# The inter-chunk product of a Mamba-2 scan: one fp32 product becomes three fp32r products of operands split by ScalarE and VectorE

## The chip, the cores and the metric

One NeuronCore of a Trainium2 chip runs the whole program in one launch. The metric is the device time of that launch in microseconds; each kernel is timed several times and the median is taken. Engines are called by the profile's names: PE (TensorE, matrix products), ACT (ScalarE), DVE (VectorE), POOL (GpSimd) and SP (SyncE, which issues the loads of the weights).

## What is computed

A decoder of two layers over 256 tokens of width 2048, all in fp32. The first layer is a Mamba-2 mixer, the second a sliding-window attention; each is followed by a squared-ReLU MLP. The change lies in the state-space scan of the mixer, which the reference does in two chunks of 128 tokens:

```python
def step(state, inp):
    xdt_c, dA_c, b_c, c_c = inp
    cs = jnp.cumsum(dA_c, axis=1)
    seg = cs[:, :, None] - cs[:, None, :]
    decay = jnp.exp(jnp.where(causal[None, :, :, None, None], seg, -jnp.inf))
    cb = jnp.einsum('bign,bjgn->bgij', c_c, b_c)
    y_intra = jnp.einsum('bgij,bijgh,bjghp->bighp', cb, decay, xdt_c)
    y_inter = jnp.einsum('bign,bghpn->bighp', c_c, state) * jnp.exp(cs)[..., None]
    to_end = jnp.exp(cs[:, -1:] - cs)
    new_state = (state * jnp.exp(cs[:, -1])[..., None, None]
                 + jnp.einsum('bjgn,bjgh,bjghp->bghpn', b_c, to_end, xdt_c))
    return new_state, y_intra + y_inter
```

With two chunks and a zero state at the start only `y_inter` of the second chunk is not zero. It is what the first token half carries into the second. There are eight groups of eight heads (64 columns each).

## The kernel before

Weights stream from HBM in chunks of 128x1024 numbers. Every fp32 product of weights is done as three fp32r products (high by high, low by high, high by low). So ACT rounds each chunk into `whi` (`split_weights`, L838) and DVE writes the rest into `wlo` (L1270); a ring of eight such slots (`RING`) runs up to six chunks ahead of PE (`LEAD`), and the raw chunks have four buffers (`RAW`). On ACT and DVE one call of `step()` splits one chunk, and the order of all other work between the steps is written out by hand in `group` of each engine. The semaphores `w_split` (chunk ready) and `w_used` (chunk used) tie the streams to PE.

The mixer goes group by group. On PE, `group(par, prev)` makes six row tiles of the current group (`row_tile(i % 2, actA)`, lines L453 and L459, into PSUM banks 0 and 1 by turns) and then a block of z columns (`column_block`, L478 to L480). Between them stands the scan of the previous group:

- behind row tile 0, `s1`: transposes of x, and C times B of the tokens (`cb`) into bank 6 (L593, L594)
- behind row tile 3, `s4_both`: the inter-chunk product `s4` (L610, 128x128 by 128x512 in fp32), then the intra-chunk products `intra(0, 5)` and `intra(1, 7)` (L602), which wait on `m_ready`
- inside the column block, the transposes of the normed result (`s67`)

Row tile 4 goes into bank 0 again, so `fill(0)` waits until DVE has taken row tile 2 out of it, in `conv_sum` of `conv(2)` (L1393).

On ACT, `cross` (L913) takes half a row tile out, `tanh` (L923) serves the silu, and `decay(c)` makes the decay matrix `em` of a token half: eight ReLUs (L940) and an exp (L944). On DVE, `d1(c)` scales x by dt (L1428, L1430) and `d1(1)` also makes `xde` (L1434), the moving operand of `s4`; `bc_out` takes `cb` out of bank 6, two masked tiles (L1440) and a copy (L1441) which is the weight of `s4`; `d23(c)` multiplies `em` by the masked `cb` (L1446) and signals `m_ready`.

The last (eighth) group's scan runs in the first block of the out projection, `slab(actA, ..., after={3: [s4], 5: [lambda: intra(1, 7)], 7: [s67]})`, beside `split_y` of DVE and ACT.

Of the kernel before, what the change touches and what calls it, by code (L numbers as in the profile page):

```python
# [23 lines left out]
F32 = mybir.dt.float32  # L24
F32R = mybir.dt.float32r
ACT = mybir.ActivationFunctionType
ALU = mybir.AluOpType
AX = mybir.AxisListType

P = 128  # L30
T = 256
NH = T // P
# [4 lines left out]
GH = 8  # L37
HD = 64
GW = GH * HD
# [90 lines left out]
def build(nc, t, out):  # L130
# [24 lines left out]
    z_tanh_done = nc.alloc_semaphore("z_tanh_done")  # L155
    xdt_ready = nc.alloc_semaphore("xdt_ready")
    m_ready = nc.alloc_semaphore("m_ready")
    y_ready = nc.alloc_semaphore("y_ready")
    y_squared = nc.alloc_semaphore("y_squared")
    rstd_ready = nc.alloc_semaphore("rstd_ready")  # L160
# [17 lines left out]
    full = [nc.alloc_semaphore(f"full{b}") for b in range(8)]  # L178
# [60 lines left out]
    def region(start, limit):  # L239
        pos = [start]  # L240

        def put(name, shape, dtype=F32):
            x = place(name, shape, dtype, pos[0])
            pos[0] += (int(np.prod(shape[1:])) * 4 + 31) // 32 * 32
            assert pos[0] <= limit, (name, pos[0] - limit)
            return x
        return put
# [6 lines left out]
    xD = put("xD", [P, NH, GW])  # L254
    xin = place("xin", [P, NH, D], F32, res_at)
    put = region(scr, end)
    xT = put("xT", [P, 2, 6, T])
    xpad = put("xpad", [P, 2, 3 + T + 1])
    xh = put("xh", [P, 2, T])
    thb = put("thb", [P, 2, T])  # L260
    yb = put("yb", [P, NH, GW])
    zs = put("zs", [P, NH, GW])
    xde = put("xde", [P, GW])
    bcb = put("bcb", [P, 3, P])
    st = put("st", [P, GW])

    put = region(y_at, y_at + KT * 2 * T * 4)
    kst = put("kst", [P, K_END])
# [71 lines left out]
    with block:  # L340
# [76 lines left out]
        def _(e):  # L417
# [187 lines left out]
                last.then_inc(full[b], C.up(full[b]))  # L605

            def s4():
                e.wait_ge(xdt_ready, C.next(xdt_ready))
                fill(4)
                e.matmul(ps[:, 4, :], bcb[:, 1, :], xde[:, :], start=True, stop=True).then_inc(full[4], C.up(full[4]))  # L610
                intra(0, 5)

            def s4_both():
# [214 lines left out]
        def _(e):  # L828
# [11 lines left out]
            def step():  # L840


                C.n[w_used] += 1
                if C.n[w_hi_done] < TOTAL and C.any(w_used, back=RING - 1 - LEAD):
                    e.wait_ge(w_used, C.now(w_used, back=RING - 1 - LEAD))
                split_weights()
# [74 lines left out]
            def tanh(i):  # L921
                e.wait_ge(conv_done, C.next(conv_done))
                e.activation(thb[:, i % 2, :], xh[:, i % 2, :], ACT.Tanh).then_inc(tanh_done, C.up(tanh_done))  # L923
# [4 lines left out]
                    e.activation(yb[:, c, :], ps[:, 2 + c, :], ACT.Tanh, scale=0.5).then_inc(  # L928
                        z_tanh_done, C.up(z_tanh_done))

            def a1():
                C.n[full[6]] += 1
                C.n[free[6]] += 1

            def decay(c, par):
                if c == 0:
                    e.wait_ge(rows_in, C.next(rows_in))
                    e.wait_ge(group_sums, C.next(group_sums))
                for h in range(GH):
                    last = e.activation(em[:, c, h * P:(h + 1) * P], csb[:, h, c * P:(c + 1) * P], ACT.Relu,  # L940
                                        bias=csg[:, par, c, h:h + 1], scale=-1.0)
                last.then_inc(clamped, C.up(clamped))
                e.wait_ge(clamped, C.now(clamped))
                e.activation(em[:, c, :], em[:, c, :], ACT.Exp, scale=-1.0).then_inc(decayed, C.up(decayed))  # L944
# [60 lines left out]
            def group(par):  # L1005
                step()
                z_tanh()
                step()
                step()
                cross(0)  # L1010
                step()
                tanh(0)
                a1()
                step()
                cross(1)
                decay(0, par)
                step()
                tanh(1)
                step()
                cross(2)  # L1020
                decay(1, par)
                step()
                tanh(2)
                step()
                cross(3)
                step()
                tanh(3)
                step()
                cross(4)
                step()  # L1030
                tanh(4)
                square(0)
                step()
                cross(5)
                step()
                tanh(5)
                square(1)
                step()
                scale_y()
                for _ in range(5):  # L1040
                    step()
# [15 lines left out]
            split_y(0, range(2))  # L1057
            z_tanh()
            split_y(0, range(2, 4))
            a1()  # L1060
            step()
            decay(0, 1)
            step()
            decay(1, 1)
            step()
# [194 lines left out]
        def _(e):  # L1260
# [12 lines left out]
            def step():  # L1273
                C.n[w_used] += 1
                split_weights()
# [160 lines left out]

            def bc_out():
                e.wait_ge(full[6], C.next(full[6]))
                for c in range(NH):
                    e.tensor_tensor(bcb[:, 2 * c, :], ps[:, 6, 2 * c * P:(2 * c + 1) * P], tri[:, :], ALU.mult)  # L1440
                e.tensor_copy(bcb[:, 1, :], ps[:, 6, P:2 * P]).then_inc(free[6], C.up(free[6]))  # L1441

            def d23(c):
                e.wait_ge(decayed, C.next(decayed))
                x = em[:, c, :].rearrange("p (h n) -> p h n", h=GH)
                e.tensor_tensor(x, x, bcb[:, 2 * c, :].unsqueeze(1).broadcast_to([P, GH, P]), ALU.mult).then_inc(  # L1446
                    m_ready, C.up(m_ready))

            def gate(c):
# [74 lines left out]
            def group(g, par):  # L1524

                step()
                e.tensor_copy(cwg[:, par, :], cw[:, bass.ds(g * 30, 30)]).then_inc(dve_step, C.up(dve_step))
                e.wait_ge(dve_step, C.now(dve_step))
                step()
                z_out()  # L1530
                step()
                conv(0, par)
                bc_out()
                step()
                d1(0, g - 1)
                step()
                conv(1, par)
                silu(0, par)
                d1(1, g - 1)
                step()  # L1540
                d23(0)
                d23(1)
                step()
                conv(2, par)
                silu(1, par)
                step()
                step()
                conv(3, par)
                silu(2, par)
                step()  # L1550
                d4()
                step()
                conv(4, par)
                silu(3, par)
                step()
                d5(g - 1)
                step()
                conv(5, par)
                silu(4, par)
                step()  # L1560
                silu(5, par)
                for _ in range(5):
                    step()
                d8(0, g - 1)
                step()
                d8(1, g - 1)
# [46 lines left out]

            g7 = NG - 1
            step()
            split_y(0, {1: bc_out})
            z_out()
            d1(0, g7)
            d1(1, g7)
            step()  # L1620
            d23(0)
            step()
            d23(1)
            step()
# [480 lines left out]
```

## Time and profile before

| what | value |
|---|---|
| time, median of 3 runs | 2387.52 us (2387.07 to 2387.99) |
| span of the profiled execution | 2386.3 us |
| PE busy | 2368.3 us (99%) |
| DVE busy | 1588.6 us (67%) |
| ACT busy | 1140.5 us (48%) |
| rate of the DMA, mean | 191 GB/s |

The span runs from the first to the last instruction of the profiled execution; the three timed runs lie 0.8 to 1.7 us above it, which is what lies around the span. A busy share says nothing of who waits for whom: for that there are the views of waits, of the chain of work, and the timelines of a stretch. In a timeline each row has the start in us from the span's start, the duration in us, engine, line, operation, output and inputs, shapes and how many instructions were merged.

### The profile page before, as it was taken

Reading aid. Unit: us, or ns where it says so; the run is one execution under the profiler, and the core shown is the slowest. Engines: PE = TensorE matmul, PEld = TensorE weight load, DVE = VectorE, ACT = ScalarE, POOL = GpSimd, SP = SyncE. Lnnn points to the kernel's source line nnn. Section 1 sums busy time; section 2 is a strip of 40 time slices with the busy share of each in tenths; the row PEclk is TensorE's granted clock in tenths of the full one; section 3 lists DMA queues with packets and bytes.
Section 4 is the critical chain, followed back from the end, with each engine's and each line's share of the span. In section 5 each row is a group of like instructions: output and inputs, shape, how many; then the busy total and the mean of one; then the engine's idle time right before and its main releaser. Section 6 shows DMA issues by size and latency. Waiting matters only on the chain.

```text
span 2386.3 us, 32914 instructions
## 1 busy us (share of the span) xinstructions
PE 2368.3 (99%) x12818; PEld 2005.7 (84%) x12818; DVE 1588.6 (67%) x2171; ACT 1140.5 (48%) x1670; POOL 40.1 (2%) x85
## 2 busy tenths in 40 slices
PE   9999999999999999999999999999999999999998
PEld 8888888888888888888888888778888888888886
DVE  7888888885568556556556577876864654655655
ACT  5555555564355344445344354554543443443441
POOL 0000000000000000000000000000000000000000
PEclk9999999999999999999999999999999999999999
DMA  8766666656567666666666646336776666666663
GB/s 233 230 195 194 188 191 190 189 169 239 193 186 235 210 187 190 198 186 187 200 186 190 199 150 209 120 122 198 201 234 189 188 198 182 194 197 189 190 196 108
DMA packets 487828, 455.11 MB, mean 191 GB/s; under 512 B 13792, under 2 KB 360080, under 8 KB 485392
## 3 DMA queue, kind: packets, MB, share of 16 engines
q1 hardware_dynamic: 484608, 433.51, 60.3%
q0 software_dynamic: 3088, 19.79, 2.3%
q8 instruction: 90, 1.47, 0.3%
q14 instruction: 42, 0.34, 0.0%
HBM read 450.55 MB, written 2.16 MB: 190 GB/s over the span
## 4 chain that ended last, share of the span: by engine, by line
PE 93%; DVE 3%; DMA 2%; ACT 1%; issue 1%; SPq 0%; POOL 0%; DVEq 0%; ACTq 0%
PE ps L453 24%; PE ps L478 16%; PE ps L480 15%; PE ps L479 15%; PE ps L459 12%; PE ps L511 2%; PE ps L509 2%; PE ps L510 2%; PE ps L530 1%; DVE wlo L1270 1%; DMA raw<-in_a_w_in 1%; ACT whi L838 1%; PE ps L746 1%; PE ps L602 1%; PE ps L716 0%
## 5 line engine op out<-in xcount | busy, mean ns | idle before, releaser
L1270 DVE TENSOR_TENSOR wlo<-raw,whi 128x1024 fp32r<-128x1024 f32 x817 | 994.3, 1222 | 656.6 <-ACT whi L838 656.1
L838 ACT ACTIVATE whi<-raw 128x1024 fp32r<-128x1024 f32 x817 | 859.4, 1056 | 853.9 <-PE ps L480 461.2
L453 PE MATMUL ps<-actA,whi 128*128 128x512 f32 x2704 | 648.2, 392 | 0.8 <-DVE wlo L1270 0.5
L453 PEld LDWEIGHTS ps<-actA,whi 128*128 128x128 f32 x2704 | 497.2, 188 | 98.4 <-issue 0.7
L478 PE MATMUL ps<-whi,actB 128*128 128x512 f32 x1056 | 412.8, 391 | 0.1
L479 PE MATMUL ps<-wlo,actB 128*128 128x512 f32 x1056 | 411.1, 389 | 0.0
L480 PE MATMUL ps<-whi,actB 128*128 128x512 f32 x1056 | 411.1, 389 | 0.0
L459 PEld LDWEIGHTS ps<-actA,wlo 128*128 128x128 f32 x2704 | 347.2, 191 | 13.4
L459 PE MATMUL ps<-actA,wlo 128*128 128x256 f32 x2704 | 351.4, 283 | 0.0
L478 PEld LDWEIGHTS ps<-whi,actB 128*128 128x128 f32 x1056 | 198.3, 188 | 43.0 <-issue 1.3
L480 PEld LDWEIGHTS ps<-whi,actB 128*128 128x128 f32 x1056 | 198.3, 188 | 41.3
L479 PEld LDWEIGHTS ps<-wlo,actB 128*128 128x128 f32 x1056 | 198.3, 188 | 40.3
L478 PE MATMUL ps<-whi,actA 128*128 128x512 f32 x544 | 216.0, 397 | 1.7 <-DVE actA L1282 1.7
L480 PE MATMUL ps<-whi,actA 128*128 128x512 f32 x544 | 212.1, 390 | 0.0
L479 PE MATMUL ps<-wlo,actA 128*128 128x512 f32 x544 | 212.1, 390 | 0.0
L478 PEld LDWEIGHTS ps<-whi,actA 128*128 128x128 f32 x544 | 102.2, 188 | 24.3 <-issue 3.2
L480 PEld LDWEIGHTS ps<-whi,actA 128*128 128x128 f32 x544 | 102.1, 188 | 21.7
L479 PEld LDWEIGHTS ps<-wlo,actA 128*128 128x128 f32 x544 | 102.3, 188 | 19.8
L852 ACT ACTIVATE actB<-fsq 128x256 fp32r<-128x256 f32 x120 | 50.2, 418 | 111.7 <-DVE fsq L1748 111.7
L1599 DVE TENSOR_TENSOR res<-ps,res 128x512 f32<-128x512 f32 x80 | 51.9, 686 | 63.0 <-PE ps L511 32.6
L923 ACT ACTIVATE thb<-xh 128x256 f32<-128x256 f32 x48 | 19.9, 415 | 125.9 <-DVE xh L1410 125.9
L1748 DVE SCALAR_TENSOR_TENSOR fsq<-fb 128x256 f32<-128x256 f32 x120 | 51.0, 425 | 4.1
(215 smaller groups left out, 1674.3 us busy)
## 6 DMA issues: line engine op xcount, KB each, us to landing
raw<-in_mlp_w SPq DMA_DIRECT2D x512, 512.0 KB, 4.2
raw<-in_a_w_in SPq DMA_DIRECT2D x162, 512.0 KB, 4.4
raw<-in_a_w_out SPq DMA_DIRECT2D x64, 512.0 KB, 4.8
raw<-in_b_w_q SPq DMA_DIRECT2D x32, 512.0 KB, 5.2
raw<-in_b_w_o SPq DMA_DIRECT2D x32, 512.0 KB, 3.9
csb<-cs_rows POOLq DMA_DIRECT2D x8, 1024.0 KB, 6.7
raw<-in_kv_w SPq DMA_DIRECT2D x16, 512.0 KB, 3.8
gb<-in_ln_g POOLq DMA_DIRECT2D x4, 1024.0 KB, 7.3
```

The lines of the kernel that those rows point to most:

```text
L453: e.matmul(ps[:, b, :], whi[:, s, k * P:(k + 1) * P], act[:, kt, :, :].rearrange("p a n -> p (a n)"), start=(kt == 0), stop=False)
L459: last = e.matmul(ps[:, b, T:2 * T], wlo[:, slots[half], k * P:(k + 1) * P], act[:, kt, 0, :], start=False, stop=(kt == KT - 1))
L478: e.matmul(ps[:, b0 + h, :], act[:, kt, 0, tk], whi[:, s, w], start=(kt == 0), stop=False)
L479: e.matmul(ps[:, b0 + h, :], act[:, kt, 0, tk], wlo[:, s, w], start=False, stop=False)
L480: last = e.matmul(ps[:, b0 + h, :], act[:, kt, 1, tk], whi[:, s, w], start=False, stop=(kt == KT - 1))
L509: e.matmul(ps[:, b0 + h, :], act[:, kt, 0, tk], hi_w, start=(kt == 0), stop=False)
L510: e.matmul(ps[:, b0 + h, :], act[:, kt, 0, tk], lo_w, start=False, stop=False)
L838: e.activation(whi[:, s, :], raw[:, r, :], ACT.Copy).then_inc(w_hi_done, C.up(w_hi_done))
L852: e.activation(dst, src, ACT.Copy).then_inc(act_hi_done, C.up(act_hi_done))
L1270: e.tensor_tensor(wlo[:, s, :], raw[:, r, :], whi[:, s, :].bitcast(F32), ALU.subtract).then_inc(w_split, C.up(w_split))
L1599: ins = e.tensor_tensor(r, ps[:, b, :], r, ALU.add)
L1748: e.scalar_tensor_tensor(fsq[:, i % 2, :], fb[:, i % 2, :], 0.0, fb[:, i % 2, :], ALU.max, ALU.mult).then_inc(f_squared, C.up(f_squared))
```

## The change

- `s4` on PE becomes three fp32r products into bank 4: `cbh` by `xeh`, `cbh` by `xel`, `cbl` by `xeh`. It waits on `xe_split` instead of `xdt_ready`.
- ACT gets `cb_hi` (high part of the 128x128 `cb`, out of PSUM bank 6) and `xe_hi` (high part of the 128x512 `xde`). In a group `cb_hi` stands ahead of `tanh(0)` and `xe_hi` behind `tanh(1)`; in the last group `xe_hi` stands behind `decay(0, 1)`.
- DVE gets `xe_lo` (the rest of `xde`, 128x512) between `d23(0)` and `d23(1)`. In `bc_out` the copy of `cb` becomes a subtraction, and it waits on `cb_hi_done`.
- In the last group `bc_out` moves from behind piece 1 of `split_y` to behind piece 3.
- Some tiles move in SBUF; `xel` lies over `xde`.

```diff
             def s4():
-                e.wait_ge(xdt_ready, C.next(xdt_ready))
+                e.wait_ge(xe_split, C.next(xe_split))
                 fill(4)
-                e.matmul(ps[:, 4, :], bcb[:, 1, :], xde[:, :], start=True, stop=True).then_inc(full[4], C.up(full[4]))
+                e.matmul(ps[:, 4, :], cbh[:, :], xeh[:, :], start=True, stop=False)
+                e.matmul(ps[:, 4, :], cbh[:, :], xel[:, :], start=False, stop=False)
+                e.matmul(ps[:, 4, :], cbl[:, :], xeh[:, :], start=False, stop=True).then_inc(full[4], C.up(full[4]))
                 intra(0, 5)
...
-            def a1():
-                C.n[full[6]] += 1
+            def cb_hi():
+                e.wait_ge(full[6], C.next(full[6]))
+                e.activation(cbh[:, :], ps[:, 6, P:2 * P], ACT.Copy).then_inc(cb_hi_done, C.up(cb_hi_done))
                 C.n[free[6]] += 1
+
+            def xe_hi():
+                e.wait_ge(xdt_ready, C.next(xdt_ready))
+                e.activation(xeh[:, :], xde[:, :], ACT.Copy).then_inc(xe_hi_done, C.up(xe_hi_done))
...
                 step()
+                cb_hi()
                 tanh(0)
-                a1()
                 step()
                 cross(1)
                 decay(0, par)
                 step()
                 tanh(1)
+                xe_hi()
                 step()
                 cross(2)
                 decay(1, par)
...
-            a1()
+            cb_hi()
             step()
             decay(0, 1)
+            xe_hi()
             step()
             decay(1, 1)
...
             def bc_out():
                 e.wait_ge(full[6], C.next(full[6]))
+                e.wait_ge(cb_hi_done, C.next(cb_hi_done))
                 for c in range(NH):
-                    e.tensor_tensor(bcb[:, 2 * c, :], ps[:, 6, 2 * c * P:(2 * c + 1) * P], tri[:, :], ALU.mult)
-                e.tensor_copy(bcb[:, 1, :], ps[:, 6, P:2 * P]).then_inc(free[6], C.up(free[6]))
+                    e.tensor_tensor(bcb[:, c, :], ps[:, 6, 2 * c * P:(2 * c + 1) * P], tri[:, :], ALU.mult)
+                e.tensor_tensor(cbl[:, :], ps[:, 6, P:2 * P], cbh[:, :].bitcast(F32), ALU.subtract).then_inc(
+                    free[6], C.up(free[6]))
+
+            def xe_lo():
+                e.wait_ge(xe_hi_done, C.next(xe_hi_done))
+                e.tensor_tensor(xel[:, :], xde[:, :], xeh[:, :].bitcast(F32), ALU.subtract).then_inc(
+                    xe_split, C.up(xe_split))
...
                 d23(0)
+                xe_lo()
                 d23(1)
...
-            split_y(0, {1: bc_out})
+            split_y(0, {3: bc_out})
             z_out()
             d1(0, g7)
             d1(1, g7)
             step()
             d23(0)
+            xe_lo()
             step()
             d23(1)
```

ACT in the first full group, from the splitting of a chunk behind `decay(0)` on, as the program issues it before (L838 is the rounding of a weight chunk, L923 `tanh`, L913 `cross`, L940 and L944 `decay(1)`; the semaphores waited for stand in brackets):

```order
L838 ACTIVATE whi<-raw 128x1024 [waits loaded1,w_used]
L923 ACTIVATE thb<-xh 128x256 [waits conv_done]
L838 ACTIVATE whi<-raw 128x1024 [waits loaded2,w_used]
L913 ACTIVATE xpad<-ps 128x256 [waits w_used]
L940 ACTIVATE em<-csb,csg 128x128 x8
L944 ACTIVATE em<-em 128x1024 [waits clamped]
L838 ACTIVATE whi<-raw 128x1024 [waits loaded3,w_used]
```

The same place now (line numbers of the changed kernel; L847 rounds a chunk, L932 is `tanh`, L947 `xe_hi`, L922 `cross`, L954 and L958 `decay(1)`):

```order
L847 ACTIVATE whi<-raw 128x1024 [waits loaded1,w_used]
L932 ACTIVATE thb<-xh 128x256 [waits conv_done]
L947 ACTIVATE xeh<-xde 128x512 [waits xdt_ready]
L847 ACTIVATE whi<-raw 128x1024 [waits loaded2,w_used]
L922 ACTIVATE xpad<-ps 128x256 [waits w_used]
L954 ACTIVATE em<-csb,csg 128x128 x8
L958 ACTIVATE em<-em 128x1024 [waits clamped]
```

One instruction has come in, and it waits for a product of DVE (`xdt_ready`); a chunk, `cross` and the whole of `decay(1)` are queued behind it.

PE in the same group before, at `s4_both` (L459 ends row tile 3, L610 is `s4`, L602 the intra-chunk products of the two token halves):

```order
L459 MATMUL ps<-actA,wlo 128x256 x16
L610 MATMUL ps<-xde,bcb 128x512 [waits free4,xdt_ready]
L602 MATMUL ps<-xdt,em 64x64 [waits free5,m_ready]
L602 MATMUL ps<-xdt,em 64x64 x15
L602 MATMUL ps<-xdt,em 64x64 [waits free7,m_ready]
```

And now:

```order
L466 MATMUL ps<-actA,wlo 128x256 x16
L617 MATMUL ps<-xeh,cbh 128x512 [waits free4,xe_split]
L618 MATMUL ps<-xel,cbh 128x512
L619 MATMUL ps<-xeh,cbl 128x512
L609 MATMUL ps<-xdt,em 64x64 [waits free5,m_ready]
L609 MATMUL ps<-xdt,em 64x64 x15
```

One product in the program's order has become three, and the first of them waits for a semaphore that DVE raises later than the old one.

## Rows read from the trace of the kernel before

**Rows 1.** The page: span, granted clock by slice, shares of the last-ending chain

```profile
span 2386.3 us, 32914 instructions
...
PEclk9999999999999999999999999999999999999999
...
PE 93%; DVE 3%; DMA 2%; ACT 1%; issue 1%; SPq 0%; POOL 0%; DVEq 0%; ACTq 0%
```

**Rows 2.** Waits of PE: who for whom, us in total, times, longest

```profile
PE ps L478 <- DVE actA L1282: 1.7, 1, 1.7
...
PE ps L453 <- DVE wlo L1270: 0.5, 1, 0.5
PE ps L453 <- DVE xpad L1393: 0.3, 1, 0.3
```

**Rows 3.** Chain of work, last group's s4: start, us, what

```profile
516.79 0.23 PE ps L480
517.03 0.86 PE ps L610 x2
```

**Rows 4.** Timeline of PE in a middle group

```profile
205.88 0.38 PE L594 MATMUL ps<-xT 128*128 128x128 f32 x2
...
222.83 1.02 PE L610 MATMUL ps<-xde,bcb 128*128 128x512 f32 x2
...
225.79 0.50 PE L453 MATMUL ps<-actA,whi 128*128 128x512 f32 x1
```

**Rows 5.** Timeline of ACT in the same group

```profile
216.63 0.40 ACT L923 ACTIVATE thb<-xh 128x256 f32<-128x256 f32 x1
216.94 1.04 ACT L838 ACTIVATE whi<-raw 128x1024 fp32r<-128x1024 f32 x1
...
220.62 1.06 ACT L944 ACTIVATE em<-em 128x1024 f32<-128x1024 f32 x1
```

**Rows 6.** Timeline of DVE in the same group

```profile
208.40 0.48 DVE L1440 TENSOR_TENSOR bcb<-ps,tri 128x128 f32<-128x128 f32 x2
...
217.13 0.68 DVE L1434 TENSOR_TENSOR xde<-xdt,te 128x512 f32<-128x512 f32 x1
...
221.71 1.23 DVE L1446 TENSOR_TENSOR em<-em,bcb 128x1024 f32<-128x1024 f32 x1 [1.62 <-ACT em L944]
222.85 1.22 DVE L1270 TENSOR_TENSOR wlo<-raw,whi 128x1024 fp32r<-128x1024 f32 x1
223.99 0.42 DVE L1393 TENSOR_TENSOR xpad<-ps,xpad 128x256 f32<-128x256 f32 x1
...
229.00 0.42 DVE L1393 TENSOR_TENSOR xpad<-ps,xpad 128x256 f32<-128x256 f32 x1
```

**Rows 7.** Chain of work, the first group that holds a scan

```profile
102.91 1.13 DVE wlo L1270
104.04 0.34 DVE xpad L1393
...
104.43 1.66 PE ps L453 x6
```

**Rows 8.** Timelines of ACT and DVE, the same group

```profile
96.91 1.04 ACT L838 ACTIVATE whi<-raw 128x1024 fp32r<-128x1024 f32 x1
...
97.19 0.68 DVE L1434 TENSOR_TENSOR xde<-xdt,te 128x512 f32<-128x512 f32 x1
```

**Rows 9.** Groups by line and form: busy us, mean ns, idle before

```profile
L852 ACT ACTIVATE actA<-hf 128x512 fp32r<-128x512 f32 x16 | 10.1, 632 | 11.0 <-DVE hf L1661 10.6
L957 ACT ACTIVATE xdt<-yb,small 128x512 f32<-128x512 f32 x16 | 10.7, 716 | 6.2 <-POOL small L1996 6.2
```

**Rows 10.** Timelines of ACT and DVE in the last group

```profile
512.27 1.04 ACT L838 ACTIVATE whi<-raw 128x1024 fp32r<-128x1024 f32 x1
...
513.13 0.68 DVE L1434 TENSOR_TENSOR xde<-xdt,te 128x512 f32<-128x512 f32 x1
...
514.86 1.22 DVE L1446 TENSOR_TENSOR em<-em,bcb 128x1024 f32<-128x1024 f32 x1
```

More of the change, by code:

```diff
@@ L157, in build @@
     m_ready = nc.alloc_semaphore("m_ready")
+    cb_hi_done = nc.alloc_semaphore("cb_hi_done")
+    xe_hi_done = nc.alloc_semaphore("xe_hi_done")
+    xe_split = nc.alloc_semaphore("xe_split")
     y_ready = nc.alloc_semaphore("y_ready")
@@ L256, in build @@
     put = region(scr, end)
+    st = put("st", [P, GW])
+    xeh = place("xeh", [P, GW], F32R, scr)
+    xde = put("xde", [P, GW])
+    xel = place("xel", [P, GW], F32R, scr + GW * 4)
     xT = put("xT", [P, 2, 6, T])
@@ L262, in build @@
     zs = put("zs", [P, NH, GW])
-    xde = put("xde", [P, GW])
-    bcb = put("bcb", [P, 3, P])
-    st = put("st", [P, GW])
+    bcb = put("bcb", [P, NH, P])
+    cbh = put("cbh", [P, P], F32R)
+    cbl = put("cbl", [P, P], F32R)
     put = region(y_at, y_at + KT * 2 * T * 4)
@@ L1445, in d23 @@
                 x = em[:, c, :].rearrange("p (h n) -> p h n", h=GH)
-                e.tensor_tensor(x, x, bcb[:, 2 * c, :].unsqueeze(1).broadcast_to([P, GH, P]), ALU.mult).then_inc(
+                e.tensor_tensor(x, x, bcb[:, c, :].unsqueeze(1).broadcast_to([P, GH, P]), ALU.mult).then_inc(
                     m_ready, C.up(m_ready))
```

## Prediction

> **What bounds the kernel now.** I read the page first. Of the chain that ended last 93% is PE, and PE is granted its full clock in every slice [rows 1]. So the kernel costs what PE issues, plus the few places where PE waits. The view of PE's waits shows how few there are [rows 2]: once 1.7 us for DVE's `split_y` at the start of the last group's scan, once 0.5 us for a weight chunk, once 0.3 us for DVE's `conv_sum` (L1393). An edit that shortens PE's own work is therefore worth its full size, and an edit on ACT or DVE costs nothing until it makes one of their results later than PE asks for it. The question is how much room each result has, so I read the timelines of a middle group, of the first group with a scan, and of the last.
>
> **What is removed on PE.** The fp32 product is recorded as two matmuls and takes 0.86 us of the chain, while an fp32r product of 512 columns takes 0.23 [rows 3]. Three of these are 0.69, so each `s4` is 0.17 us shorter, and the eight of them 1.4 us. I take the rows' price for the three, since they have the shape of L480; a price that is certain from below is none (0 us saved) and from above 0.23 each, as if one of them vanished into the change of weights.
>
> **What is added on ACT.** `cb_hi` reads `cb` out of PSUM. In the middle group PE has it ready at 206.26 (205.88 + 0.38) [rows 4] and DVE asks for it only at 208.40, in `bc_out` [rows 6]. A copy of 128x128 is smaller than the 0.40 us of `tanh` over 128x256 [rows 5], so 1.7 us of room is left, and it costs nothing. The subtraction that takes the place of the copy in `bc_out` has the shape of the two L1440 beside it, 0.48 us for two; I cost the exchange at nothing, at most 0.1 us.
>
> `xe_hi` is another matter. It waits for `xde` (L1434), and ACT's queue is in order: a weight chunk, `cross(2)` and the whole of `decay(1)` stand behind it. Before, ACT began that chunk (L838) at 216.94, while `xde` is ready only at 217.81 (217.13 + 0.68) [rows 5, 6]. A hand-over between ACT and DVE takes 0.03 us (the exp ends at 221.68, L1446 starts at 221.71 [rows 5, 6]). The copy itself is like L852 from SBUF to fp32r, 128x512, 0.63 us [rows 9], of which 0.09 overlaps the next instruction (`tanh` begins at 216.63, takes 0.40, and the next begins at 216.94). So the chunk begins at 217.81 + 0.03 + 0.54 = 218.38, 1.44 us later. The copy with a scale of the same shape, L957, is 0.72 [rows 9]; the cost could be that, or as little as 0.45 if the overlap were twice as large, and the delay 1.35 to 1.53.
>
> **Who waits for that.** Everything behind it moves by 1.44: the exp of `decay(1)` from 221.68 to 223.12, DVE's L1446, then the weight split L1270, then `conv_sum(2)` (L1393), which ended at 224.41 (223.99 + 0.42) and now ends at 225.85. On DVE these follow one another with no room [rows 6]. PE asks for bank 0, which `conv_sum(2)` empties, at row tile 4, at 225.79 [rows 4]. With 0.05 us from DVE to PE (L1393 ends at 104.38, PE starts at 104.43 [rows 7]) the room was 225.79 - 224.41 - 0.05 = 1.33 us. So PE starts row tile 4 at 225.90, 0.11 us later than before, and the 0.17 won at `s4` just before is lost inside this wait. The bounds of the copy make it 0.02 to 0.20. `xe_lo` on DVE is hidden: it fits into the idle 1.62 us before L1446 [rows 6], and PE needs `xel` only at 222.83 [rows 4]. Between the first scan and the last, the eighth, lie six such groups of the same pattern: 6 x 0.11 = 0.7 us.
>
> **The first group with a scan** has no room: there the chain of work itself runs over `decay(1)`, L1446, L1270 and L1393 into row tile 4 [rows 7]. The same sum gives 97.19 + 0.68 + 0.03 + 0.54 = 98.44 against 96.91 before [rows 8], 1.53 us later, and all of it falls on PE. Its `s4` saving is lost too, since PE then waits longer at the same place.
>
> **The last group.** `xde` is ready at 513.81, and ACT's chunk, which began at 512.27 [rows 10], falls 2.1 us back, plus what `bc_out` behind piece 3 puts in front of `z_out` and `d1` on DVE (three instructions, 0 to 0.6 us). Behind it is `decay(1)`, whose product `intra(1, 7)` stands two chunks, 24 products of 0.23 or 5.4 us, behind `s4`, so this is hidden. What is not hidden is `xe_lo`: it follows L1446, which ends at 516.08 [rows 10], so it ends at 516.7 to 517.3, where PE takes up `s4` at 517.03 [rows 3]. A wait of 0 to 0.4 us against a saving of 0.17: I take +0.1.
>
> **The sum.** 1.53 + 0.66 + 0.1 = +2.3 us on a span of 2386.3 [rows 1]. The timed runs lie 1.2 us above that span in the median, so 2387.5 + 2.3 = 2389.8 us. That is 0.1% and less than the 0.2% (4.8 us) from which a measurement of this kernel tells a difference.
>
> **Rivals.**
>
> (a) *The stall never reaches PE, and the saving stays.* If ACT's queue has more room than I count, for instance because `xe_hi` starts nearer to the end of `tanh(1)`, PE wins 0.17 at each of eight `s4`: 2387.5 - 1.4 = 2386.1. For it speaks that in the middle groups only 0.11 us decides; against it that the first group is on the chain. A mix (middle groups win, first loses) gives 2388. Together 0.22.
>
> (b) *Slower than can be overlooked: DVE's `bc_out` waits for ACT's `cb_hi`.* If ACT comes to `cb_hi` late, `d1` and `xde` come later by as much, and with them `xe_hi`, `decay(1)`, `conv_sum(2)` and row tile 4, in all seven groups. With the forecast at +2.3, a further delay of (4.8 - 2.3) / 7 = 0.36 us in each group decides it. Half a microsecond would give 2389.8 + 3.5 = 2393.3. Against it stand the 1.7 us of room [rows 4, 6]. The same price holds for anything else that adds to the chain, up to the next asker: row tile 5 comes 5.5 us after row tile 4 (16 x 0.23 and 16 of half the width), at about 231.3, and `conv_sum(3)` ends at 229.42 [rows 6], or 230.9 with the delay, so 0.4 us are left there. Chance 0.09.
>
> (c) *The change does not do what it says: a pass costs what half the fp32 product does.* Then three passes take 3 x 0.43 = 1.29 us, 0.43 more than before. In the middle groups PE comes to row tile 4 at 226.22, past the 225.90 of DVE, so the loss is 0.43 there, 1.53 in the first, 0.43 and some wait in the last: 2.6 + 1.5 + 0.6 = 4.7, 2392.2. Against it, every L480 of the same shape is 0.23 [rows 3]. Chance 0.03.
>
> (d) *The clock.* A mechanism of this kernel would be that after the new wait of 1.5 us in the first group the granted clock falls to 1.2 GHz for one row tile; its 5.5 us would take twice that: 2389.8 + 5.5 = 2395.3. Against it: before, PE waited 1.7 us at one place [rows 2] and the granted clock shows 9 in all forty slices [rows 1]. Chance 0.02. The Trainium skill (Perfetto Trace Analysis, Matmul Optimizations) says that TensorE scales its power with its use, so that matmuls have to be issued back to back; by that rule a kernel that trades PE work for PE waits stands to lose. The trace does not bear it out at waits of this length.
>
> **How the numbers follow.** The forecast has 0.64. It lies within 0.2%, as does (a) and most of (c); (b) and (d) are slower, and a little of the forecast's own tail is (0.01). For faster by over 0.2% I find no mechanism, since all that PE can win is 1.4 us; 0.02 is for what I overlooked. So faster 0.02, same 0.86, slower 0.12. The range reaches from (a), 2386.0, to the border of (b), 2393.0.
>
> **What would show it.** In the trace of the changed kernel: three matmuls of 0.23 us spacing at `s4`; ACT's copy `xeh<-xde` beginning 0.03 us after `xde` ends, with ACT idle 0.8 us before it; in the middle groups PE idle some 0.3 us before row tile 4, released by `xpad` of DVE, which PE's waits did not show there before; in the first group about 1.8 us of it. If these waits are absent, (a) holds. If DVE idles before `bcb`, released by ACT's `cbh`, it is (b). The prediction is wrong if PE shows waits for `xe_split` in middle groups, or a weight chunk that comes late because its split stood behind the stalled chunk.

## The result, and the profile after

The changed kernel takes 2393.49 us in the median (2391.09 to 2395.36, 12 runs) against 2387.98 (2387.07 to 2389.46, 12 runs) of the kernel before: a ratio of 1.0021, with a 95% interval of 1.0014 to 1.0028. It is 5.5 us slower, a little over the 4.8 us that the prediction named as 0.2%; the prediction had 2.3 us. The median lies half a microsecond above the predicted range, but the kernel before also measures 0.46 us more here, in 12 runs, than the 2387.52 of three runs that the range was built on: as a difference, 5.5 us is just the distance from 2387.52 to the range's upper end. Two things stand out beside the median. The profiled execution, with a span of 2390.7 us, is 4.4 longer than that of before, so a typical run has about 1 us more than the trace explains. (A timed run lies 1.8 us above its own span, 2392.51 against 2390.7 here; the 0.8 to 1.7 us named before the prediction set timed runs against the span of another execution.) And the runs scatter more: 4.3 us from lowest to highest, against 2.4. That is a weak sign, since longer series of the kernel before (26 to 33 runs, below) span 3.7 to 4.3.

The waits of PE in the changed kernel (L460 is a row tile's product, L609 an intra-chunk product, L485 the column block, L537 the transposes; us in total, times, longest):

```profile
PE ps L460 <- DVE xpad L1409: 2.0, 7, 0.3
PE ps L609 <- DVE em L1469: 1.7, 1, 1.7
PE ps L485 <- DVE actA L1298: 1.4, 1, 1.4
PE ps L537 <- DMA xin<-in_x: 1.2, 2, 1.0
PE ps L537 <- DVE yT L1496: 1.2, 1, 1.2
```

The first row is the forecast one: row tile 4 now waits for `conv_sum(2)` seven times instead of once [rows 2]. The second is the first group with a scan. The last, for `yT`, was not forecast. The same middle group as in [rows 4 to 6], PE first, after the change:

```profile
225.00 0.40 PE L617 MATMUL ps<-xeh,cbh 128*128 128x512 f32 x1
225.24 0.40 PE L618 MATMUL ps<-xel,cbh 128*128 128x512 f32 x1
225.47 0.40 PE L619 MATMUL ps<-xeh,cbl 128*128 128x512 f32 x1
225.79 2.08 PE L609 MATMUL ps<-xdt,em 128*64 128x64 f32 x64
228.16 1.19 PE L460 MATMUL ps<-actA,whi 128*128 128x512 f32 x4 [0.28 <-DVE xpad L1409]
```

```profile
218.80 0.40 ACT L932 ACTIVATE thb<-xh 128x256 f32<-128x256 f32 x1
220.02 0.63 ACT L947 ACTIVATE xeh<-xde 128x512 fp32r<-128x512 f32 x1 [0.82 <-DVE xde L1450]
220.56 1.05 ACT L847 ACTIVATE whi<-raw 128x1024 fp32r<-128x1024 f32 x1
...
224.25 1.06 ACT L958 ACTIVATE em<-em 128x1024 f32<-128x1024 f32 x1
```

From the first product of `s4` to the first of L609 it is 0.79 us instead of 0.95, the gain of 0.16. ACT stands idle for 0.82 us in front of the copy and takes 0.54 for it, as worked out. Then PE idles 0.28 us in front of row tile 4, and the stretch from `s4` to row tile 4 is 3.16 us, where it was 2.96 (222.83 to 225.79 [rows 4]): 0.20 lost. Matched product by product outside `s4`, the lag of PE behind the kernel before grows by 0.18 in each of the six groups.

The first group with a scan, as the chain of work has it (compare [rows 7]):

```profile
97.74 0.61 DVE xde L1450
98.35 0.02 issue
98.37 0.02 ACT xeh L947
98.40 0.52 issue
98.91 1.05 ACT whi L847
99.96 0.27 ACT xpad L922
100.22 2.35 ACT em L954 x8
...
103.69 1.22 DVE em L1469
104.91 1.14 DVE wlo L1286
106.05 0.34 DVE xpad L1409
106.39 0.04 issue
106.44 1.66 PE ps L460 x6
```

The new copy and DVE's `xde` ahead of it are on the chain, with `decay(1)` behind them. Row tile 4 starts at 106.44 where it started at 104.43. But this execution's `s4` already starts 0.49 us late (101.26 against 100.78), and that is not the change: 0.30 are from waits for the first loads, and the rest is one weight chunk that ACT got 0.55 us later (91.54 against 90.99), by which `xel` was 0.2 us late. So 1.52 belongs to the change. Other profiles of kernels with the same stall (the splitting alone, `d8` ahead, the turn eased, one idle time filled) gain 1.3 to 1.6 us of lag between row tile 3 and row tile 4 of this group, loads included, where this one gains 1.7.

To see where the 4.4 us of the two traces lie, I matched PE's products one by one, outside `s4`, and followed how far the changed kernel lags (`yT`, the transposed result of a group, and `actA`, the split operand of the out projection, are what PE asks DVE for at the turn to the last group). The steps, worked out from the start times of the two traces:

| place | lag added, us | forecast |
|---|---|---|
| loads, up to the first `s4` | +0.49 | 0 |
| first group with a scan | +1.52 | +1.53 |
| six middle groups | 6 x 0.18 = +1.07 | +0.66 |
| turn to the last group, `s1` waits for `yT` | +1.32 | not named |
| the same turn, the wait for `actA` is shorter | -0.29 | 0 |
| last `s4` | +0.22 | +0.1 |
| sum at the last scan | +4.33 | +2.3 |

### The profile page after: what moved, and what is told of

Same layout as the page of the kernel before. It is cut to its first block, busy times and chain, and to the rows that moved or that the text cites. A ratio compares the mean times of both kernels' runs of the same rounds, so it can differ in the third digit from the quotient of the medians.

```text
span 2390.7 us, 32968 instructions
## 1 busy us (share of the span) xinstructions
PE 2368.8 (99%) x12826; PEld 2007.5 (84%) x12826; DVE 1593.6 (67%) x2179; ACT 1146.7 (48%) x1686; POOL 40.5 (2%) x85
## 4 chain that ended last, share of the span: by engine, by line
PE 90%; DVE 4%; ACT 2%; issue 1%; DMA 1%; SPq 0%; DVEq 0%; POOL 0%; ACTq 0%
PE ps L460 23%; PE ps L485 16%; PE ps L487 15%; PE ps L486 15%; PE ps L466 12%; PE ps L518 2%; PE ps L516 2%; PE ps L517 2%; PE ps L537 1%; DVE wlo L1286 1%; ACT whi L847 1%; DMA raw<-in_a_w_in 1%; ACT em L954 1%; DVE xh L1423 1%; PE ps L755 1%
## 5 line engine op out<-in xcount | busy, mean ns | idle before, releaser
L847 ACT ACTIVATE whi<-raw 128x1024 fp32r<-128x1024 f32 x817 | 859.3, 1056 | 848.7 <-PE ps L487 453.1
L460 PE MATMUL ps<-actA,whi 128*128 128x512 f32 x2704 | 648.1, 391 | 2.5 <-DVE xpad L1409 2.0
L460 PEld LDWEIGHTS ps<-actA,whi 128*128 128x128 f32 x2704 | 497.2, 188 | 100.5 <-DVE wlo L1286 2.5
L485 PE MATMUL ps<-whi,actB 128*128 128x512 f32 x1056 | 412.7, 391 | 0.1
L485 PEld LDWEIGHTS ps<-whi,actB 128*128 128x128 f32 x1056 | 198.2, 188 | 42.9 <-issue 1.3
L485 PE MATMUL ps<-whi,actA 128*128 128x512 f32 x544 | 215.9, 397 | 1.4 <-DVE actA L1298 1.4
L485 PEld LDWEIGHTS ps<-whi,actA 128*128 128x128 f32 x544 | 102.1, 188 | 24.1 <-issue 2.9
L932 ACT ACTIVATE thb<-xh 128x256 f32<-128x256 f32 x48 | 19.9, 416 | 121.3 <-DVE xh L1426 121.3
```

The costliest lines, as they stand in the source:

```text
L460: e.matmul(ps[:, b, :], whi[:, s, k * P:(k + 1) * P], act[:, kt, :, :].rearrange("p a n -> p (a n)"), start=(kt == 0), stop=False)
L485: e.matmul(ps[:, b0 + h, :], act[:, kt, 0, tk], whi[:, s, w], start=(kt == 0), stop=False)
L847: e.activation(whi[:, s, :], raw[:, r, :], ACT.Copy).then_inc(w_hi_done, C.up(w_hi_done))
```

## Experiments

The ratios are taken against runs of the kernel before in the same round of measurements: 2388.34 us in the median of 33 runs beside the copy behind the step, the products alone, the splitting alone and `d8` ahead; 2388.13 (26 runs) beside the early `xde`, the doubled copy, the one idle time filled and the turn eased; 2388.78 (27 runs) beside the last three. So two bare medians of different rounds compare to within some 0.8 us only.

**xe_hi behind the step.** The copy goes behind the weight chunk, so that ACT does something while `xde` is made. In the last group, not shown, it is moved in the same way.

```diff
                 tanh(1)
-                xe_hi()
                 step()
+                xe_hi()
                 cross(2)
                 decay(1, par)
```

> The changed kernel with xe_hi moved behind the next weight chunk on ACT (in the last group too), so that in the first seven scans ACT no longer stands idle for xde. The result stays the reference's. Theory (in-order stall): what cost the time is the 0.8 us for which ACT's queue stood still with decay(1) behind it. Then decay(1) comes 0.54 us later than before instead of 1.44, inside the 1.33 us of room of the middle groups: PE shows no wait before row tile 4 there and wins 0.17 in each of six; the first group loses 0.54, the turn to the last group some 0.3, the last 0.2. Sum about 0, 2388 us. Rival (the three products or the extra work itself cost it): the time stays at 2393 us, and the waits before row tile 4 stay.

Measured: 2388.84 us, ratio 1.0002 (0.9993 to 1.0011). The loss is gone. In the timeline of ACT the copy follows the chunk without a gap, and PE takes up row tile 4 at 225.46 with no wait:

```profile
216.76 1.04 ACT L847 ACTIVATE whi<-raw 128x1024 fp32r<-128x1024 f32 x1
217.71 0.61 ACT L947 ACTIVATE xeh<-xde 128x512 fp32r<-128x512 f32 x1
218.22 0.36 ACT L922 ACTIVATE xpad<-ps 128x256 f32<-128x256 f32 x1
```

```profile
223.44 2.08 PE L609 MATMUL ps<-xdt,em 128*64 128x64 f32 x64
225.46 1.89 PE L460 MATMUL ps<-actA,whi 128*128 128x512 f32 x7
```

The same instructions, one place further on in one queue, are worth 4.6 us of the medians (2393.49 to 2388.84), or 4.5 by the ratios. So it is not the extra work and not the three products that cost the time, but where the copy stands in ACT's queue, with its wait at the head.

**The three products alone.** The kernel before, with three products of operands that lie ready (tiles of `actA`). They stand in for the real ones, so `s4` leaves out its true product.

```diff
-                e.matmul(ps[:, 4, :], bcb[:, 1, :], xde[:, :], start=True, stop=True).then_inc(full[4], C.up(full[4]))
+                for i in range(3):
+                    last = e.matmul(ps[:, 4, :], actA[:, 0, 0, 0:P], actA[:, 1 + i % 2, :, :].rearrange("p a n -> p (a n)"),
+                                    start=(i == 0), stop=(i == 2))
+                last.then_inc(full[4], C.up(full[4]))
```

> The kernel before with s4 as three fp32r products of operands that lie ready (tiles of actA), and no splitting on ACT or DVE: the product is not the one that the reference asks for, everything else is as before. Theory: this is the edit's gain alone. Each s4 is 0.15 to 0.17 us shorter; it is lost in the first group, where PE waits for decay(1) anyway, and kept in the other seven: -1.1 us, about 2386.9, no wait before row tile 4 but in the first group. Rival (three passes cost as much as or more than the two recorded fp32 passes): 0 or a loss.

Measured: 2386.78 us, ratio 0.9994 (0.9985 to 1.0003). The interval does not tell it from no change, but its trace shows the gain: in the chain of a middle group `s4` takes 0.69 us for three products where it took 0.86 for two [rows 3].

```profile
221.21 1.91 PE ps L459 x16
223.12 0.69 PE ps L611 x3
223.82 2.01 PE ps L602 x64
225.83 0.43 PE ps L453
```

The lag falls by 0.16 in each middle group.

**The splitting alone.** All of ACT's and DVE's new work, and one fp32 product of the high parts; it leaves out the low parts.

```diff
-                e.matmul(ps[:, 4, :], cbh[:, :], xeh[:, :], start=True, stop=False)
-                e.matmul(ps[:, 4, :], cbh[:, :], xel[:, :], start=False, stop=False)
-                e.matmul(ps[:, 4, :], cbl[:, :], xeh[:, :], start=False, stop=True).then_inc(full[4], C.up(full[4]))
+                e.matmul(ps[:, 4, :], cbh[:, :].bitcast(F32), xeh[:, :].bitcast(F32), start=True, stop=True).then_inc(
+                    full[4], C.up(full[4]))
```

> The changed kernel with all splitting, but s4 is again one fp32 product, of the high parts only (the low parts are left out of it). Theory: row tile 4 waits for conv_sum(2), whose time hangs on row tile 1 and ACT's queue, not on s4; so the saved 0.16 us per group is worth nothing where it stands, and this kernel takes as long as the changed one in the first seven scans, within 0.2 us, and 0.16 longer in the last: 2393.5. Rival (saving and loss add up): it is longer by 8 x 0.16 = 1.3 us, 2394.8.

Measured: 2393.70 us, ratio 1.0020 (1.0011 to 1.0029), as long as with the three products (2393.49). In its trace each middle group adds 0.19 us of lag, with the long product, where the changed kernel adds 0.18 with the three short ones. What `s4` saves in front of a wait that does not hang on it is worth nothing.

This kernel's profile also caught something else. Behind the turn to the last group PE stood idle 0.69 and then 2.67 us, and the granted clock fell to half 0.3 us after it took up work again. By stretches (us, PE busy with its count, granted clock, share and rate of the DMA):

```profile
506.00:511.00 5.00, 1.72 (x10) 0.99 0.67 234
511.00:514.30 3.30, 3.30 (x10) 0.50 0.35 120
514.30:518.00 3.70, 3.70 (x18) 1.00 0.02 4
```

At 0.50, the lower level of 1.2 GHz, products of 512 columns start every 0.43 us instead of every 0.23, eight of them in a row: 1.6 us lost. That is what rival (d) of the prediction describes, at another place and at a smaller price.

**xe_hi twice.** One more copy, behind the completion of the first.

```diff
+                e.activation(xeh[:, :], xde[:, :], ACT.Copy).then_inc(dosed, C.up(dosed))
+                e.wait_ge(dosed, C.now(dosed))
                 e.activation(xeh[:, :], xde[:, :], ACT.Copy).then_inc(xe_hi_done, C.up(xe_hi_done))
```

> The changed kernel with xe_hi done twice in a row, the second copy behind the first one's completion, which holds ACT's queue 0.66 us longer. The result stays the reference's. Theory (row tile 4 hangs on ACT's queue in all seven groups): each of the seven loses 0.66 more, 4.6 us, and the turn to the last group some more where DVE's lag is 0.66 longer and PE's idle time longer: 2393.5 + 4.6 + 0 to 2, that is 2398 to 2400. Rival (the middle groups lose because of something else at s4): only the first group loses the 0.66: 2394.2.

Measured: 2398.63 us in five runs, ratio 1.0047 (1.0033 to 1.0061), 5.1 us over the changed kernel. In the middle groups the lag grows by 0.84 instead of 0.18, just the dose of 0.66. PE's waits show where it goes, to `em` and to `xpad`, seven times each:

```profile
PE ps L610 <- DVE em L1472: 4.3, 7, 2.3
PE ps L461 <- DVE xpad L1412: 2.7, 7, 0.4
```

With this dose PE has no room left in any of the seven groups. In the second scan it waits for `em` as well:

```profile
228.69 1.15 PE L610 MATMUL ps<-xdt,em 128*64 128x64 f32 x32 [0.33 <-DVE em L1472]
```

**xde made early.** `xde` needs only the first half of `xdt`, so it can be made two row tiles earlier, and `xe_hi` falls where ACT waits for PE. (`xde_early` holds the two products of DVE that `d1` then leaves out.)

```diff
                 conv(0, par)
+                xde_early(g - 1)
                 bc_out()
...
                 cb_hi()
                 tanh(0)
+                xe_hi()
                 step()
...
                 tanh(1)
-                xe_hi()
```

> The changed kernel with xde made right behind conv(0) on DVE (it needs only the first token half of xdt) and xe_hi right behind tanh(0) on ACT, where ACT waits for PE anyway. The result stays the reference's. Theory (the loss is the stall of ACT's queue ahead of decay(1), and what follows from DVE's lag behind PE): decay(1) comes as early as before the change, PE wins 0.16 in each middle group and the turn to the last group costs what it cost before: 6 x 0.16 = 1.0 won, 0.1 lost in the first group and 0.2 in the last, 2387.6 us, and no wait before row tile 4. Rival (extra work on ACT and DVE costs as such): as the kernel with xe_hi behind the step or slower, 2388.8 or more.

Measured: 2388.32 us, ratio 1.0001 (0.9992 to 1.0010), 0.7 us above what I expected and no different from the kernel before. In the trace the rest is as expected: ACT is idle before and behind the copy, so it costs the queue nothing,

```profile
208.25 0.42 ACT L932 ACTIVATE thb<-xh 128x256 f32<-128x256 f32 x1 [1.93 <-DVE xh L1426]
209.67 0.64 ACT L947 ACTIVATE xeh<-xde 128x512 fp32r<-128x512 f32 x1 [0.99 <-DVE xde L1447]
210.76 1.06 ACT L847 ACTIVATE whi<-raw 128x1024 fp32r<-128x1024 f32 x1 [0.45 <-PE ps L466]
```

and PE's lag falls to 1.2 us below zero; this profiled span is 2385.1, the shortest of the changed versions up to here. The median lies 1.4 us above the profiled run (2386.91, the fastest of the eleven). So a gap between a typical run and a profiled one is there also in a kernel without the stall, whose longest wait in the scans is 1.2 us.

**d8 ahead of the chunk.** The wait for `yT` at the turn: DVE frees bank 5 in `d8(1)`, behind the split of a weight chunk that waits for a load.

```diff
                 d8(0, g - 1)
-                step()
                 d8(1, g - 1)
+                step()
```

> The changed kernel with d8(1) ahead of the weight chunk that stood between d8(0) and d8(1) on DVE, in every group. The result stays the reference's. Theory: the second part of the loss is the turn to the last group, where PE waits 1.2 us for d8(1) (yT), because DVE is 1.25 us late since row tile 4 and its split of a chunk waits for a load just there. With d8(1) ahead of that chunk, the wait for yT goes: 1.2 us less, some 2392.0, and the times scatter less. Rival: the wait moves on, to split_y and the load (PE's wait for actA grows from 1.4 to 2.6), and nothing is won.

Measured: 2393.43 us, ratio 1.0021 (1.0012 to 1.0030). Nothing is won in the median, against 1.2 us expected. In the trace, which is that of the fastest of its runs (2390.59), the wait for `yT` is gone, and PE's wait for `actA` has grown, as the rival said, though only from 1.4 to 2.1:

```profile
PE ps L485 <- DVE actA L1298: 2.1, 1, 2.1
```

Behind `d8` stands the same chunk, and `split_y` behind it. The edit was too small for what it was to test.

**The turn eased.** So `split_y` too goes ahead of the chunk, on both engines.

```diff
-            step()
+            C.n[w_used] += 1
+            e.wait_ge(w_used, C.now(w_used, back=RING - 1 - LEAD))
             split_y(0, range(2))
+            split_weights()
             z_tanh()
...
-            step()
-            split_y(0, {3: bc_out})
+            split_y(0, {1: step, 3: bc_out})
```

> The changed kernel with the turn to the last group freed of the weight load: d8(1) ahead of the chunk on DVE in every group, and in the last group split_y pieces 0 and 1 ahead of the chunk on both ACT and DVE. The result stays the reference's. Theory (half of the loss lies at this turn, where DVE and ACT sit behind a load while PE asks for yT and actA): the wait for yT goes, that for actA falls below 1.7 us, the clock holds; left is the first group's 1.5 and six times 0.18: 2388.3 + 2.6 + 0.2, less up to 1 that the turn gains over the kernel before: 2390 to 2391. Rival (the turn does not matter, the chunk is missed later by PE): 2393.5, with PE waiting for a weight chunk behind the turn.

Measured: 2391.64 us, ratio 1.0014 (1.0005 to 1.0023), 1.8 us below the changed kernel and 0.6 above what I expected. At the turn the lag falls by 1.18 instead of growing by 1.03, but 1.1 of it goes again at the last `s4`, where PE waits for `xel` of DVE. The two turns are not quite alike, since PE came to this one 1.4 us later: this profile caught a fall of the clock behind the first group with a scan, where PE had idled 1.64 us. The lower level holds from 106.6 to 110.0, so that the second row mixes both:

```profile
102.00:106.00 4.00, 2.23 (x64) 1.00 0.66 221
106.00:109.40 3.40, 3.21 (x8) 0.59 0.75 238
109.40:113.00 3.60, 3.60 (x22) 0.91 0.62 180
```

It cost 1.6 us, like the other one.

**One idle time filled.** Products that nobody reads, where PE waits for `actA`.

```diff
             s1(1)
+            for _ in range(8):
+                e.matmul(ps[:, 7, 0:P], ident[:, :], ident[:, :], start=True, stop=True)
             slab(actA,
```

> The changed kernel with eight idle fp32 products of the unit matrix (into bank 7, read by nobody) between s1 and the out projection of the last group, 1.7 us of PE, where PE waits for split_y. The result stays the reference's. Theory (part of the loss, about 1 us of the median, is the granted clock: in many runs it falls to 1.2 GHz for one stretch after PE has stood idle twice around the turn to the last group; one profile showed 3.4 us at that level, worth 1.7 us): the products fill PE's idle time, the clock holds in every run, and the runs draw together at the changed kernel's faster ones, 2392.3 to 2392.8, with none above 2394. Rival (the scatter is from the loads): the scatter stays, and the products cost 0 to 0.3 us: 2393.5 to 2393.8.

Measured: 2393.26 us, ratio 1.0022 (1.0013 to 1.0032), with 2391.79 to 2395.52 about the same scatter. The expectation was missed; the first place was still open.

**Both idle times filled.** The same, and eight more between the two intra-chunk products of the first group with a scan.

```diff
+            def s4_both_filled():
+                s4()
+                emptied(7)
+                for _ in range(8):
+                    e.matmul(ps[:, 7, 0:P], ident[:, :], ident[:, :], start=True, stop=True)
+                intra(1, 7)
```

> The changed kernel with eight idle fp32 products of the unit matrix (into bank 7, overwritten or read by nobody) in both places where PE stands idle for more than 1 us: between the two intra-chunk products of the first group with a scan, and between s1 and the out projection in the last. The result stays the reference's. Theory (the median lies about 1 us above the profiled run because the granted clock falls in part of the runs after one of the two idle times; two profiles of other kernels showed it, one behind the first place, one behind the second): with both filled the clock holds, the median falls to that of the runs without a fall, 2392.4, and the slowest of 11 stays under 2394. Rival (the rest of the scatter is the weight loads at the start and at the turn): median 2393.3 and the same scatter as with one place filled.

Measured: 2392.71 us, 2391.87 to 2393.52, ratio 1.0017 (1.0008 to 1.0026). The slowest run is below 2394, and the scatter of 1.7 us is less than half of the changed kernel's 4.3; the median falls by some 0.7, or by 1.6 if each is taken against the kernel before of its round (3.9 over 2388.78, 5.5 over 2387.98), with intervals that overlap. The kernel that gives PE more to do has lost its longest times. That fits the clock; what share of the median it has is taken up below.

**The turn without the change, and with it.** Two kernels with the same eased turn, and the chunk behind `d23(0)` in the last group: one is the kernel before, the other has the three products with the early `xde`.

```diff
             d1(1, g7)
-            step()
             d23(0)
+            step()
             step()
             d23(1)
```

> The kernel before, without any of the change, with the turn to the last group eased: d8(1) ahead of the chunk on DVE in every group; in the last group split_y pieces 0 and 1 ahead of the chunk on ACT and DVE, and the chunk behind d23(0). The result stays the reference's. It is the reference point for the next one: PE's wait of 1.7 us for actA falls to some 0.7, 1 us won, 2387.2. Rival (the order of DVE at the turn gives the gain back at s4, where PE would wait for em): 2388.1.

> The changed kernel with xde made early and xe_hi in ACT's idle time, and with the same eased turn to the last group. The result stays the reference's. Theory: the gain of the three products is kept in the middle groups (1.0 us), and 1 us is won at the turn: 2388.1 - 2.0 = 2386.1, the lowest of all. Rival (at the last s4 PE waits for xel and gives back the turn's gain, as it did in the eased kernel with the late xde, where it waited 1.1 us): 2387.2.

Measured: 2386.71 us, ratio 0.9991 (0.9982 to 1.0000), without the change; 2385.64 us, ratio 0.9986 (0.9977 to 0.9995), with it. The second is the fastest of all and clear of the kernel before. From the one to the other it is 1.1 us in the medians, about what the six middle groups give (0.9), though the two intervals overlap. The rival of the second kernel had a part: PE waits 0.6 us for `xel` at the last `s4`.

```profile
PE ps L617 <- DVE xel L1470: 0.6, 1, 0.6
```

The first kernel's rival, a wait for `em` at the last scan, is not in its trace. There is a wait for `em` in the first scan instead, 1.4 us long, where the kernel before had 0.1:

```profile
PE ps L602 <- DVE em L1448: 1.4, 1, 1.4
```

Nothing of the change is in this kernel, and up to there its order is that of the kernel before. What differed is a load: ACT got a chunk of weights at 92.52 where it had it at 90.99, and its queue, `decay(1)` with it, came 1.5 us later. The second kernel's profile has the same chunk at 92.38; in the others that wait for it there it comes between 90.3 and 91.6. So a late load can cost an execution over 1 us at this place.

## Why the prediction was right or wrong

**The gain.** 0.17 us per `s4` was forecast, 0.15 to 0.17 is there in every trace. That it would be worth nothing in front of row tile 4 is shown by the splitting alone, as slow as the whole change.

**The stall of ACT's queue.** Right in place, order and size: ACT idle for 0.82 us, 0.54 for the copy, `decay(1)` and `conv_sum(2)` later by as much, the wait on `xpad` in all seven groups. The kernel with the copy one place further on and the one with it twice show that it is the cause, and the doubled one that the loss follows the delay one to one. The first group with a scan lost 1.52 where 1.53 was forecast; that the two agree to 0.01 is in part luck, as the other profiles of this stall differ by 0.3 among themselves.

**The middle groups.** Forecast 0.11 each, measured 0.18. The term that was mis-sized is the hand-over from DVE to PE. I took 0.05 us from the first group. The six middle groups show 0.13, from the end of `conv_sum(2)` at 228.03 to the product at 228.16, and in the chain of the changed kernel:

```profile
227.69 0.35 DVE xpad L1409
228.04 0.12 issue
228.16 0.95 PE ps L460 x3
```

The six middle groups run in a loop of the program and the first does not, but the loop alone is not the reason: in the kernel with the doubled copy PE's waits for `em` (L610) end 0.05 us after DVE in the same loop, and outside of it other waits of PE end 0.15 (`wlo`) and 0.26 us (`actA`) after DVE. What makes the 0.08 at row tile 4 stays open.

**The turn to the last group.** This is the step that failed. The prediction priced only `s4` and `decay(1)` in "The last group", at +0.1 (measured +0.22), and took it that a stall which PE has paid at row tile 4 is over. It is not: since row tile 4 DVE and ACT stay behind PE by the 1.44 of the stall less what PE itself lost, about 1.25 us. Within the loop that costs nothing, for there is idle time until the next scan. In the last group the chain behind it runs over a load of the out projection's weights, which starts when DVE has freed a raw buffer, and PE asks for bank 5 and for `actA` just there. Its chain, after the change:

```profile
498.64 1.23 DVE wlo L1286
499.87 0.02 issue
499.88 6.32 DMA raw<-in_a_w_out
...
506.28 1.06 ACT whi L847
507.34 1.31 ACT actA L861 x2
```

And before it:

```profile
495.55 6.53 DMA raw<-in_a_w_out
```

The load starts 4.33 us later than before, while PE lags by only 3.05: DVE's 1.28 us behind PE are handed on to the load. The prediction had such a thing among its signs of being wrong (a weight chunk that comes late because of the stalled one), but no price for it in the sum. It cost 1.03 us net in this trace. The eased turn took 1.8 us off the median, and in the kernel without any stall (early `xde`) the wait for `yT` is 0.2 us instead of 1.2. The direction holds over the profiles, the size does not: with the stall the turn cost 1.03, 1.85 (splitting alone) and 0.31 us (doubled copy), without it 0.18 (copy behind the step) and -0.15 (early `xde`). These are single executions, and the loads at the turn differ from one to the next.

**The rest of the median.** Some 1 us of the 5.5 is in no trace of the changed kernel, and 0.49 of what is in its trace is from loads. The prediction gave 0.02 to a fall of the clock behind a wait of this length (d), since the wait of 1.7 us before the change was followed by none [rows 1, 2]. One profiled execution without a fall was weak evidence. Of the seven profiles with a wait of 1.5 us or more at these places, the kernel before among them, two showed a fall to 0.50, one behind 1.64 us of idle PE and one behind 0.69 and 2.67, for 3.4 us each and worth 1.6. The Trainium skill (Perfetto Trace Analysis, Matmul Optimizations) says that TensorE scales its power with its use; these two stretches agree, and I had argued it away.

The record also has the mean granted clock of every run, to three places. One fall of 3.4 us to half takes 0.0007 off it: in the traces it is 0.9977 in the two profiles with a fall and 0.9982 to 0.9988 in the others, which differ in how long the clock is at half at their very end. So a run at 0.999 has had no fall, and a run at 0.998 may have had one. Of the changed kernel's twelve runs five have 0.999, with a median of 2392.51, the profiled run's own time, and seven 0.998, with a median of 2394.23: 1.7 us apart, the price of one fall. With both idle times filled there is no such distance (2392.44 and 2392.74). That speaks for the clock as the larger part of the missing 1 us. It is not shown: runs at 0.998 need not have had a fall, and the kernel with the three products alone, whose longest wait at these places is 0.9 us in its profile, scatters by 4.0 us, again with the slower runs at 0.998. The rival is the loads. PE's lag ahead of the first scan lies between -0.54 and +0.37 us over the profiles, and a late chunk cost the kernel with the eased turn and without the change over 1 us; two of the thirteen profiles have such a chunk. What share each has stays open.

**The rivals.** (a), that the stall stays hidden, is refuted by the seven waits. (b), `bc_out` waiting for `cb_hi`, did not happen: in no group does DVE idle in front of `bcb`. (c) is refuted by the 0.69 us for three products.

## What to carry to other kernels

An instruction that waits at the head of an in-order queue costs what is queued behind it, not what it does. Before a copy is put into ACT's or DVE's order, read when its input is ready and what stands behind it; one place further on, or an input made earlier, was worth all or nearly all of the loss here. A stall that has been paid once leaves its engine late, so follow the lag on to the next place without idle time, above all across a change of stage. And a saving on the bounding engine counts only if the next thing it asks for is ready that much earlier.

## What the runs showed of the hardware

- After PE had waited 1.64 us in one profile, and 0.69 and 2.67 us in another, the granted clock fell to 1.2 GHz for 3.4 us, at a cost of 1.6 us each; after longest waits of 1.7, 1.7, 1.7, 2.1 and 2.3 us in five others (the kernel before, the changed kernel, one idle time filled, `d8` ahead, the doubled copy) it did not. The length of the wait alone does not decide it.
- A hand-over from DVE to PE took 0.05 to 0.06 us at `em`, inside the program's loop and outside, and at `yT`; at the first product of row tile 4 it took 0.05 to 0.06 outside the loop and 0.13 inside, the same in all six groups to 0.002 us; at `wlo` it was 0.05 or 0.15, and at `actA` 0.25 to 0.26. Between DVE and ACT it was 0.03 us in the median.
- An fp32 product of 512 columns took 0.86 us of PE's chain, three fp32r products 0.69.
